# Retention in pairs of heads with a norm on turned tiles, and the second mixer's latent attention in pairs of heads

## The reference, cut to what matters

```
y_inner = (q k^T * dmask) v ;  y_cross = xi * q (decayed state)        # chunks of 128 tokens
y  = (y_inner + y_cross)                                               # [512, 8, 64]
mu, var over the 64 columns of a head
yn = (y - mu) * rsqrt(var + EPS) * g_ret_norm
out = silu(gate) * yn
```

```
s = q k^T * 96**-0.5, causal ;  p = softmax(s) ;  out = p v            # blocks of 128 queries
```

## Time and profile before

| | us |
|---|---|
| median of 3 runs | 3269.73 |
| lowest, highest | 3262.85, 3292.15 |
| profiled execution | 3272.07 |
| its span (first to last instruction) | 3270.3 |
| PE busy | 2922.2 (89%) |
| DVE busy | 2032.6 (62%) |
| ACT busy | 1072.9 (33%) |

### The profile page before, as it was taken

How to read it: one execution, slowest core, us unless ns; L and a number is a source line. 1 busy time by engine, 2 the same in 40 slices (tenths; PEclk the granted TensorE clock), 3 DMA queues, 4 the chain that set the end, 5 groups by cost and what they waited for, 6 DMA issues and landing times. The chain is left out here.

```text
span 3270.3 us, 37720 instructions
## 1 busy us (share of the span) xinstructions
PE 2922.2 (89%) x14130; PEld 2475.4 (76%) x14130; DVE 2032.6 (62%) x3425; ACT 1072.9 (33%) x1555; POOL 807.3 (25%) x548
## 2 busy tenths in 40 slices
PE   4999997987679789997896879999989999999998
PEld 4788875965467677886774668999978888888776
DVE  6673745544933243234534428989758888898887
ACT  1221214232332232223213433555533333333333
POOL 0000000001001000000000023666756676676221
PEclk9999998998579889998997889999999999999999
DMA  7774722201023223331200113556688888888995
GB/s 264 247 230 151 252 84 90 62 20 33 1 54 94 72 78 102 90 101 54 94 5 17 52 54 104 169 185 205 202 305 315 315 322 319 301 309 305 350 349 216
DMA packets 298413, 537.37 MB, mean 164 GB/s; under 512 B 12584, under 2 KB 193036, under 8 KB 280460
## 3 DMA queue, kind: packets, MB, share of 16 engines
q1 hardware_dynamic: 211696, 375.72, 33.9%
q0 software_dynamic: 36864, 134.23, 11.5%
q10 hardware_dynamic: 49692, 25.28, 2.8%
HBM read 496.39 MB, written 38.80 MB: 164 GB/s over the span
## 5 line engine op out<-in xcount | busy, mean ns | idle before, releaser
L170 PE MATMUL ps<-query_h_hi,expert_u_hi 128*128 128x384 f32 (+1 forms) x1152 | 399.2, 347 | 4.7 <-ACT expert_u_hi L2263 4.6
L170 PE MATMUL ps<-query_h_lo,expert_u_hi 128*128 128x384 f32 (+1 forms) x1152 | 395.4, 343 | 0.0
L2013 POOL TENSOR_TENSOR expert_u_lo<-feat,expert_u_hi 128x1024 fp32r<-128x1024 f32 x144 | 354.8, 2465 | 142.9 <-ACT expert_u_hi L2263 141.4
L170 PE MATMUL ps<-expert_v_hi,expert_w_hi 128*128 128x512 f32 x768 | 305.0, 397 | 31.3 <-DVE expert_w_lo L2169 28.8
L170 PE MATMUL ps<-expert_v_hi,expert_w_lo 128*128 128x512 f32 x768 | 301.8, 393 | 0.0
L170 PE MATMUL ps<-expert_v_lo,expert_w_hi 128*128 128x512 f32 x768 | 301.6, 393 | 0.0
L170 PE MATMUL ps<-ffn_h_hi,ffn_w_hi 128*128 128x512 f32 x704 | 278.2, 395 | 19.0 <-PEq L557 17.9
L170 PE MATMUL ps<-ffn_h_lo,ffn_w_hi 128*128 128x512 f32 x704 | 275.9, 392 | 0.0
L170 PE MATMUL ps<-ffn_h_hi,ffn_w_lo 128*128 128x512 f32 x704 | 275.8, 392 | 0.0
L218 DVE TENSOR_TENSOR ffn_w_lo<-ffn_w_raw,ffn_w_hi 128x2048 fp32r<-128x2048 f32 x66 | 151.1, 2290 | 163.4 <-ACT ffn_w_hi L214 163.4
L2174 DVE TENSOR_TENSOR expert_v_lo<-peer_s,expert_v_hi 128x1024 fp32r<-128x1024 f32 x128 | 189.4, 1480 | 74.8 <-ACT expert_v_hi L2271 74.7
(11 more groups left out here) (434 smaller groups left out, 6303.7 us busy)
## 6 DMA issues: line engine op xcount, KB each, us to landing
feat<-in_expert_u_blocks SPq DMA_DIRECT2D x64, 1024.0 KB
peer_s<-in_expert_v_blocks SPq DMA_DIRECT2D x64, 1024.0 KB
gate_rows<-expert_gates SPq DMA_DIRECT2D x32, 768.0 KB
ffn_w_raw<-in_w_gate SPq DMA_DIRECT2D x44, 512.0 KB, 4.0
ffn_w_raw<-in_w_up SPq DMA_DIRECT2D x44, 512.0 KB, 5.2
ffn_w_raw<-in_w_down SPq DMA_DIRECT2D x22, 1024.0 KB, 4.9
gate_rows<-in_w_mod SPq DMA_DIRECT2D x18, 1024.0 KB, 5.4
in_w_raw<-in_w_in SPq DMA_DIRECT2D x16, 1024.0 KB, 5.2
```

Source lines behind the costliest of these rows:

```text
L170: return nc.tensor.matmul(out, lhsT, rhs, start=start, stop=stop, skip_group_check=True)
L2013: nc.gpsimd.tensor_tensor(u_lo[:, n % 2, :, :], u_raw[:, n // 2 % 2, n % 2, :, :], u_hi[:, n % 2, :, :], ALU.subtract).then_inc(u_lo_done, 1)
```

## The change

- The retention works on pairs of heads (2p, 2p+1). The scores of the two heads are issued in turn, one on rows 0 to 63 and one on rows 64 to 127, into two different banks. The value product has `v` as the stationary side and the masked scores as moving columns, so the output comes turned: features on partitions, both heads of the pair in one bank, on partitions 0 to 63 and 64 to 127.
- The norm is computed on that turned output and in the same block: a product with a constant matrix subtracts the head's mean (`centre`), ACT squares it, four products of 2 moving columns sum the squares (`variance`), ACT takes the root, DVE the reciprocal, eight products with a broadcast column as the stationary side spread it over the features (`spread_roots`), and DVE multiplies twice, by the root and by weight and gate.
- The gate is turned together with q and k (12 jobs instead of 8), Silu is applied to the turned gate, and the stages `stage_retention_norm` and `stage_turn` "reto" are gone. The two constant matrices (256 columns) are loaded at the start of the block.
- `latent_attention` of the second mixer is replaced by `latent_pairs`, which calls `stage_attention_pairs` with items of (i+1)*P columns. With it go `warm_up`, and the stage `stage_turn` "mlao". The first mixer's `latent_attention` stays.

```diff
-def stage_retention(nc, b, q_t, k_t, v, y):
+def stage_retention(nc, b, q_t, k_t, v, gate_t, weight, out_t, const_pack):
...
+        def score_ps(j, half):
+            return b.ps[:, 2 * (j % 2) + half, 0:S - j * P]
...
+                sp.dma_start(heads[:, :], const_pack[:, at:at + 2 * P]).then_inc(heads_in, 16)
...
+                def scores(p, tiles):
+                    for j in tiles:
+                        for half in range(2):
+                            n = p * 2 * TT + 2 * j + half
+                            at = DH * half
+                            if n >= 4:
+                                pe.wait_ge(masked, n - 3)
+                            mm(nc, score_ps(j, half), k_t[at:at + DH, p, j * P:(j + 1) * P], q_t[at:at + DH, p, j * P:S],
+                               True, True).then_inc(score_up, 1)
+
+                def values(p):
+                    pe.wait_ge(masked, (p + 1) * 2 * TT)
+                    if p >= 2:
+                        pe.wait_ge(normed, p - 1)
                     for j in range(TT):
...
+                        for half in range(2):
+                            h, at = 2 * p + half, DH * half
+                            ins = mm(nc, b.ps[at:at + DH, 4 + p % 2, j * P:S], v[:, j, h * DH:(h + 1) * DH],
+                                     kept[:, p % 2, half, j, 0:S - j * P], j == 0, j == TT - 1)
...
+                def centre(p):
+                    pe.wait_ge(heads_in, 16)
+                    pe.wait_ge(y_out, p + 1)
+                    if p >= 2:
+                        pe.wait_ge(kept_centred, p - 1)
+                    mm(nc, b.ps[:, 6 + p % 2, :], heads[:, P:2 * P], y[:, p % 2, :], True, True).then_inc(centred, 1)
+
+                def variance(p):
+                    pe.wait_ge(squared, p + 1)
                     for i in range(TT):
...
+                        ins = mm(nc, b.ps[:, 4 + p % 2, 2 * i:2 * i + 2], sq[:, p % 2, i * P:(i + 1) * P], heads[:, 0:P:DH],
+                                 True, True)
+                    ins.then_inc(var_up, 1)
+
+                def spread_roots(p):
+                    pe.wait_ge(inverted, p + 1)
+                    for i in range(TT):
+                        for half in range(2):
+                            at, n = DH * half, 2 * i + half
+                            ins = mm(nc, b.ps[at:at + DH, 4 + p % 2, i * P:(i + 1) * P],
+                                     root[:, p % 2, n:n + 1].to_broadcast([P, DH]), b.const("identity"), True, True)
+                    ins.then_inc(spread, 1)
+
+                for s in range(NP + 3):
+                    if s >= 3:
+                        variance(s - 3)
+                    if s < NP:
+                        scores(s, (0, 1))
+                    if s >= 3:
+                        spread_roots(s - 3)
+                    if s < NP:
+                        scores(s, (2, 3))
+                    if 0 <= s - 2 < NP:
+                        centre(s - 2)
+                    if 0 <= s - 1 < NP:
+                        values(s - 1)
...
+                for s in range(NP + 3):
+                    p = s - 3
+                    if p >= 0:
+                        dve.wait_ge(rooted, p + 1)
+                        nc.vector.reciprocal(root[:, p % 2, :], root[:, p % 2, :]).then_inc(inverted, 1)
+                    if s < NP:
+                        if s >= 2:
+                            dve.wait_ge(y_up, s - 1)
+                        masks(s, 0)
+                        masks(s, 1)
+                    if p >= 0:
+                        dve.wait_ge(kept_centred, p + 1)
+                        dve.wait_ge(spread, p + 1)
+                        nc.vector.tensor_tensor(scaled[:, p % 2, :], y[:, p % 2, :], b.ps[:, 4 + p % 2, :],
+                                                ALU.mult).then_inc(normed, 1)
+                        dve.wait_ge(normed, p + 1)
+                        dve.wait_ge(gate_done, 1)
+                        nc.vector.scalar_tensor_tensor(out_t[:, p, :], scaled[:, p % 2, :], weight[:, p:p + 1],
+                                                       gate_t[:, p, :], ALU.mult, ALU.mult)
+                    if s < NP:
+                        masks(s, 2)
+                        masks(s, 3)
...
+                nc.scalar.activation(gate_t[:, :, :], gate_t[:, :, :], ACT.Silu).then_inc(gate_done, 1)
...
+def latent_pairs(nc, b, tag, q_t, k_t, v, bias, o_t):
+
+    items = []
+    for i in range(TT):
+        for h in range(HEADS):
+            w = (i + 1) * P
+            at = DV * (h % 2)
+            items.append(([(0, w, q_t[:, h, i * P:w], k_t[:, h, 0:w])], bias(i),
+                          [v[:, k, h * DV:(h + 1) * DV] for k in range(i + 1)], o_t[at:at + DV, h // 2, i * P:w]))
+    stage_attention_pairs(nc, b, tag, items, S, DQ ** -0.5)
...
-            stage_retention_norm(nc, b, rq, rg[:, :, :])
-            g = VEC_AT["g_ret_norm_2"]
-            stage_turn(nc, b, "reto", [(lambda i, n=n: rg[:, i, n * P:(n + 1) * P], P, y_t[:, 4 + n, :],
-                                        b.vec[:, g + n:g + n + 1]) for n in range(4)])
...
-                latent_attention(nc, b, "mla", q_t, k_t, v, lambda i: bias[:, S - (i + 1) * P:S], y_t[:, 0:4, :])
+                latent_pairs(nc, b, "mla", q_t, k_t, v, lambda i: bias[:, S - (i + 1) * P:S], y_t[:, 0:4, :])
```

More of the change, by code:

```diff
@@ L1383, in stage_attention_pairs, with turn_ps @@
         flat = b.ps[:, :, :].rearrange("p k n -> p (k n)")
-        turn_ps = flat[:, 2048:2048 + width]
+        size = [bias.shape[-1] for _p, bias, _v, _d in items]
+        def turn_ps(n):
+            return flat[:, 2048:2048 + size[n]]
         def score_ps(n):
-            return flat[:, (n % 2) * 1024:(n % 2) * 1024 + width]
+            return flat[:, (n % 2) * 1024:(n % 2) * 1024 + size[n]]
         def value_ps(n):
@@ L1711, in _, with masks @@
             @block.vector
             def _(dve):
[L1713 to L1720 removed]
+                def masks(p, j):
+                    w = S - j * P
+                    for half in range(2):
+                        dve.wait_ge(score_up, p * 2 * TT + 2 * j + half + 1)
+                        nc.vector.tensor_tensor(kept[:, p % 2, half, j, 0:w], score_ps(j, half), mask[:, 0:w],
+                                                ALU.mult).then_inc(masked, 1)
@@ new lines, in _ @@
+                nc.scalar.activation(gate_t[:, :, :], gate_t[:, :, :], ACT.Silu).then_inc(gate_done, 1)
+                for s in range(NP + 3):
+                    if s >= 3:
+                        p = s - 3
+                        act.wait_ge(var_up, p + 1)
+                        if p >= 2:
+                            act.wait_ge(spread, p - 1)
+                        nc.scalar.activation(root[:, p % 2, :], b.ps[:, 4 + p % 2, 0:2 * TT], ACT.Sqrt,
+                                             bias=b.const("eps")).then_inc(rooted, 1)
+                    if 0 <= s - 2 < NP:
+                        p = s - 2
+                        act.wait_ge(centred, p + 1)
+                        if p >= 2:
+                            act.wait_ge(var_up, p - 1)
+                        nc.scalar.activation(sq[:, p % 2, :], b.ps[:, 6 + p % 2, :], ACT.Square).then_inc(squared, 1)
+                        nc.scalar.activation(y[:, p % 2, :], b.ps[:, 6 + p % 2, :], ACT.Copy).then_inc(kept_centred, 1)
+                    if 0 <= s - 1 < NP:
+                        p = s - 1
+                        act.wait_ge(y_up, p + 1)
+                        if p >= 2:
+                            act.wait_ge(normed, p - 1)
+                        nc.scalar.activation(y[:, p % 2, :], b.ps[:, 4 + p % 2, :], ACT.Copy).then_inc(y_out, 1)
```

113 lines of the change are left out of this document (39 added, 74 removed).

## The result

The changed kernel takes 3248.85 us (median of 11 runs, 3237.76 to 3251.47), the kernel before 3272.25 beside it (11 runs): a ratio of 0.991 by the means of the runs, with an interval of 0.9882 to 0.9937 (the medians alone give 0.993). The forecast was 3241, the range 3228 to 3260. The profiled execution took 3250.86, its span 3248.6.

The account below looks back on a forecast made before the run. PE, then a chain on DVE, bound the retention, and PE the latent attention. 16.8 - 1.2 - 1.5 + 14 + 0.5 = 28.6 us saved took the profiled 3272.07 to 3243.5, so median 3241; range 3228 to 3260.

Parts of the forecast that it names:

- the rival of 3252: Both stages: half the gain lost to exclusive value halves, mode changes of 0.2, or a lasting low clock; 14 to 20 us, chance 0.20.
- the forecast's case: Whole kernel: both touched stages gain, with part lost to array mode changes and low clock; 28.6 us less, chance 0.52.
- terms for mode and clock: Retention: 1.2 us lost to PE's changes of array mode (5 at most), 1.5 to a clock dip (0 to 6).
- Fill: Retention's start, pairs 0 and 1: two score blocks and values, 9.95 us.
- step 2: Retention: a pair's scores 3.8, centre, and values 2.2, together 6.85 us.
- step 3: Retention: variance 0.9, scores 3.8 with root and spread inside, centre 0.86, values 2.2, together 7.75 us.
- step 4: Retention: variance 0.9, root 0.95, spread 0.9, centre 0.85, values 2.2, together 5.85 us.
- The shared bank: Retention values: both halves write one bank without excluding each other, no cost taken; otherwise 3.1 us a pair, 12 in all.
- Behind the retention: 1734.8 to 1742.6, formerly at half clock, may run partly at full clock: 0.5 us gained, at most 2.
- Latent attention: Second mixer: pairs paced by a PE-DVE loop, 17.5 us less at full clock, 3.5 lost to low clock: 14 less.
- The slower rival: Both stages: the clock stays at 0.50 throughout, making the kernel 12.5 us slower, 3282; chance 0.04.
- The rival in which the clock stays up: Both stages at full clock: 35 us less, 3235; chance 0.22.

Follow-up runs that it names:

- halves in turn: Changed kernel with the retention's two heads of a pair issued one after the other instead of interleaved; retention 47.44 us, ratio 0.9952 to the changed kernel.
- masks on three engines: Changed kernel with DVE masking even heads, ACT copying odd heads' scores, POOL masking them, and Silu moved earlier; retention 40.33 us, ratio 0.9916.
- the run that holds the clock: Changed kernel plus two unread 256-column products in each of the first four 128-key latent pairs; latent attention 55.57 us, ratio 0.9916.
- two runs of the table: Changed kernel with a pair's heads issued one after the other, and with masks shared by DVE, ACT and POOL; retention 47.44 and 40.33 us.

## Why the prediction was right, and where it was off

The median lies 7.8 us above the forecast, inside the range and within 1% of before, which was the likeliest outcome. By numbers it is nearer to the rival of 3252; by mechanism it is the forecast's case.

- **What bounds.** Right for this change: each half gave what its stages gave, and the four stages gave 26.3 of the 28.6 forecast. That a microsecond saved in a stage is a microsecond of the end holds only within 2 to 3 us, though: the stages behind the retention gave back 0.8 here, and in the runs with halves in turn and with masks on three engines they took 2.6 us less than in the changed kernel. And part of the nearness is luck: the retention with its turn gave 1.3 us more than forecast with its terms for mode and clock, and the stages behind it 1.3 less. Of the other 5.5 us, 2.5 are the kernel before, which ran 2.5 slower here than in the runs shown, and 3 lie outside the touched stages: the medians differ by 23.4, the stages by 26.3.
- **Retention.** Turn 1.75 more, as forecast. 39.75 forecast before the terms for mode and clock, 41.15 measured. Fill 9.89 (9.95), step 2 7.28 (6.85), step 3 8.46 (7.75), step 4 6.04 (5.85), the rest 9.45 (9.35). The excess of 1.4 sits in the steps that change between scores, centre and values: the score block is 0.12 longer in step 2 and 0.3 in step 3, the centre takes 1.05 instead of 0.86 until the values start. That fits the 1.2 for changes of mode. No run took the changes away alone, so it is argued, not shown. The 0.19 behind the centre is within the 0.1 to 0.2 that I had estimated for one change, and all of the excess, 1.4, is under a third of the 5 us that I had taken as the far end.
- **The shared bank.** Right: the order by heads made values 1.5 us a pair longer. The rows of contiguous operands and of column halves were the ones to go by the earlier trace rows, not the strided scores: in the run with masks on three engines a pair's 16 score passes, 5120 columns, take 2.87 us, less than the 4.3 of their columns.
- **Clock in the retention.** 1.5 forecast, and none of it came: it fell only 1.2 us before the stage's end. It came right behind instead, see the next point. With a faster loop it did come in the stage, about 0.9 at the last spread.
- **Behind the retention.** 0.5 gained forecast, 0.8 lost. The forecast took the low clock to end sooner, counted from the stage's start; it ended later, after 9.0 us (1722.2) instead of 7.8 (1742.6), and `uq2`'s products take 19.95 us instead of 19.39. The second low stretch, from 1739.3, lasts 10.2 us instead of 6.9, with PE busy 4.05 of them.
- **Latent attention.** This is the term that was most mis-sized: 14 forecast, 11.65 measured. Pairs of 512 keys at 4.4 (measured 4.45) and a wait of 0.63 for the copy were right, and the 96-row scores did not run together: four passes take 1.72 us (1801.10 to the turn's start at 1802.82), 4 x 0.43. The full-clock sum was 54.0, and the run that holds the clock takes 55.57: 0.7 in the pairs (45.9 between 16 bias passes, 45.2 forecast), 0.9 at start and end. The low clock costs 4.3 by the filled run, not 3.5. It fell where forecast, in the light pairs, lasted 17.1 instead of 23.9, and ended at 1776.8, in the last pair of 256 keys, as forecast. Pairs of 256 and 384 keys took 2.57 and 3.51 at full clock (2.5, 3.5 forecast), 256 keys 3.67 at half (3.6).
- **The slower rival** did not come near: no stretch of 0.50 went through a stage. The rival in which the clock stays up is shown reachable, by order or by filling, but not by the change as it stands.

## What to carry to other kernels

Count a stage with two engines in turn by its loop, not by either engine's busy time (4.45 us for a pair of 512 keys here, in which DVE waits 1.35 and PE 0.63), and signal each half of a pair: a wait for both made a pair 0.6 us longer here. Put products that are to hold the clock up where PE waits in light work, or run the heavy work first (55.57 and 53.21 us for the stage here, against 59.92); ahead of the work they made the stage 5.6 us longer and gave nothing back. When work moves to a third engine, read what already stands in that engine's queue: one Silu of 3.2 us with its table held the fill back by 1.9. And read the next stages with the one that was changed: a low clock that ended 6 us later there cost 2.6 us, as much as Silu's new place had given.

## What the runs showed of the hardware that I had not expected

- The clock stayed low for long over a loop with products of 64 moving columns, though PE's records have almost no gap: 23.9 of 23.9 us busy at 0.50, and 27.09 of 27.30 without the warm-up. With pairs that stream wider columns full clock came back after 17.1 us, after 10.2 with the signal.
- Two column halves that accumulate into one bank run together: 16 passes in 2.38 us against 3.86 in turn.
- What an edit does to the clock can show in the next stage: `uq2`'s products, which no run edits, take 17.43 us in two runs of the table and 19.95 to 20.01 in the two others, by how long the low clock reaches into them.
- Stages that no edit touches differ between profiled executions of near-identical programs: the stretch of the first mixer from the turn "lat1" to the gated stage takes 207.62 us in the kernel before and in the one without warm-up, 199.9 to 202.6 in all the others. It goes with the clock: 140.8 us of it are at 0.50 in those two, 129.0 in the changed kernel (202.62 us) and 122.4 to 122.7 in the rest. So 5.0 of the 6.1 us by which the part ahead of the touched stages differs are this stretch. Why the clock differs there stays open.
